# Where the mixer steps stand beside the expert pairs: a hybrid mLSTM, attention and PEER layer on one core

## The chip, the core and the metric

The kernel runs on one core of one Trainium2 chip. The metric is device time in microseconds. The kernel before took 3650.06 us (median of 3 runs, 3642.83 to 3653.0). All data is float32.

## The reference

One layer is computed for 128 context tokens and 1024 latent tokens (model width 1024), which are nine tiles of 128 tokens. For each token x:

```
h  = modulate(rmsnorm(x), c)
x1 = x + gate1 * [ mLSTM(h) | attention(h) ] @ w_out      # mLSTM: 4 heads of 128, both directions; attention: 8 heads of 64
h2 = modulate(rmsnorm(x1), c)
q  = h2 @ w_q                                             # 1024 x 2048: 8 heads, two halves of 128
sa, sb = q[:, half 0] @ sub_a.T, q[:, half 1] @ sub_b.T   # 128 scores each
(va, ia), (vb, ib) = top_k(sa, 16), top_k(sb, 16)
top, pos = top_k(va + vb over all 256 sums, 16)           # 16 experts a head, 128 a token
e  = ia[..] * 128 + ib[..];  gates = softmax(top)
y  = x1 + gate2 * sum over the 128 experts of  gates * gelu(h2 . u[e]) * v[e]
```

The attention of a latent token goes to its neighbours within 128 tokens and to 128 cached context keys. The mLSTM runs over the latent tiles forwards and backwards, with a state that is carried from tile to tile. u and v are tables of 16384 rows of 1024; 147,456 rows of each are gathered, 1208 MB in all, and this is most of the memory traffic.

## The kernel before, in words

There are three programs one after the other. `conditioning` and `project_in` make the modulation and h @ w_in for all tiles, and put q, k, v and the heads into DRAM scratch. `mix_and_experts` (from line 658) does the rest. It is the only one that the change touches, apart from four semaphores that it takes over from `conditioning`.

`mix_and_experts` has one program for each engine. Every program is written by the same generator `drive` out of five kinds of pieces, so that the order of the pieces is the same on all engines, and each engine works in its own order:

- `mlstm()`: 18 units (two directions, nine tiles), each in three steps, and a last round of three: 57 cell steps. A unit loads q and k turned, k, v and the sums of the gates (`load_cell`). The sums are broadcast to all partitions and land in the same buffer `ew` in which ACT then makes their exponentials.
- `mixer(t)`: 15 steps (`SUBS`) for a tile. In steps 0 to 8 even steps write the scores of two heads and weigh the values of two (PE), and odd steps take the minimum (DVE), the exponential (ACT) and the turn (PE) of two heads. Step 4 adds the mLSTM outputs of both directions and squares them (POOL), steps 5 to 8 norm them. Step 9 turns the mix, steps 10 to 13 multiply by w_out, and steps 12 and 14 add to x and give x1. Step 14 stores x1.
- `route(t)`: 51 steps for a tile: the norm of x1, sixteen query products with chunks of w_q in two halves, the scores of the sub-keys, and then on DVE the top 16 of 16 lists of 128 and of 8 lists of 256, and the expert numbers and gates. `choose` does this in two parts of 4 heads; after each part the semaphore `s_route` rises and POOL may fetch the experts of these heads.
- `pair(t, r)`: 64 pairs for a tile. A pair is two gathers by POOL (a row of u and v for every token), two dot products with h2 on DVE, gelu and weights on ACT, and the weighted sum of the v rows on PE. The ring holds 8 gathers, so POOL issues the gathers of pair n+4 when PE has done pair n.
- `begin()`: waits until all mLSTM units are stored, then issues the first gathers.

In the lead-in `drive` issues 6 cell steps, the 15 steps of the context mixer with 7 cell steps, and 34 routing steps of tile 0 with 44 cell steps (`PART`, `cells_beside`). After `begin`, after each `pair(t, r)` it issues `pace(t, r)` routing steps and a mixer step if `due(t, r)` says so. Before, the mixers of tiles 1 to 8 (120 steps) take 49 steps in expert tile 0, 41 in tile 1 (17 of them beside its pairs 0 to 27) and 30 in tile 2, never more than one a pair. Expert tile 0 has 51 routing steps.

w_q comes in chunks of 512 KB. For the first three tiles (`STREAMED`) every tile's queries read 16 chunks that SP loads anew: into four buffers in the first half of tile 0, into two after that. At pair 30 of tile 2 (`WQ_AT`), when all mixers are done, w_q is loaded whole (8.39 MB) into the space that the mixers leave, and all later queries read it there.

## Time and profile before

| | |
|---|---|
| median of 3 runs | 3650.06 us |
| the profiled execution: time, span | 3663.39 us, 3661.7 us |
| first gather issued | 630.4 us |
| first expert pair of tiles 0, 1, 2, 3, 4 on DVE | 639.3, 1007.1, 1377.3, 1727.6, 2048.4 us |
| PE, DVE, ACT, POOL busy | 72%, 67%, 27%, 40% of the span |
| gathers: 1208.03 MB | 79.0% of the time of 16 DMA engines |
| all DMA | 1368.53 MB, mean 374 GB/s |

Matmuls and the other instructions are named by engine, line and tiles (`fx_acc<-fx_ring`, the expert matmul, reads the gathered rows); a buffer's number is left out. A float32 matmul of 512 columns shows as two records. Busy time is that of an engine's instructions, the DMA share is the mean over 16 DMA engines, and the clock is that which TensorE was granted, as a share of the full 2.4 GHz. Stages are cut at the first dot product that ends a tile's pair; pairs 28 of tiles 1 and 2 are at 1161.3 and 1530.8 us.

### The profile page before, as it was taken

To read this page: it belongs to the slowest core of one execution; us is meant where nothing else is said; L and a number is where in the kernel's file an instruction comes from. 1 tells how busy PE (TensorE), PEld (TensorE's weight loads), DVE (VectorE), ACT (ScalarE), POOL (GpSimd) and SP (SyncE) were. 2 spreads that over 40 slices of the span, in tenths; PEclk is the share of its full clock that TensorE was granted. 3 is DMA by queue.
4 is the path that set the end of the run, shared out by engine and by line. 5 is a ranking of instruction groups with operands and counts; after the bars stand their busy time and mean duration, and the time that the engine had idled before them with its cause. 6 is when DMAs were issued, how large, how long until landed. Compare 5 with 4: busy or idle time off the path is not lost.

```text
span 3661.7 us, 30563 instructions
## 1 busy us (share of the span) xinstructions
PE 2650.2 (72%) x9522; PEld 1018.7 (28%) x9522; DVE 2444.6 (67%) x5512; ACT 984.9 (27%) x2685; POOL 1462.5 (40%) x1298
## 2 busy tenths in 40 slices
PE   7999786888868888766576667557656755675555
PEld 3455455333323333322122112112211211221111
DVE  3665446857685768648867667686766768676655
ACT  1223233443433244412122122112212211221111
POOL 0110023443553444534444444444444444444443
PEclk9999888899888989988788779778977977987777
DMA  7222467999999999999999999999999999999998
GB/s 300 94 99 95 164 201 229 403 416 425 394 427 402 409 391 416 416 424 413 427 427 423 427 423 427 420 421 427 417 427 417 427 419 424 426 418 426 417 427 366
DMA packets 233359, 1368.53 MB, mean 374 GB/s; under 512 B 25422, under 2 KB 45530, under 8 KB 84714
## 3 DMA queue, kind: packets, MB, share of 16 engines
q0 software_dynamic: 165888, 1208.03, 79.0%
q1 hardware_dynamic: 60104, 138.71, 10.5%
q10 hardware_dynamic: 7204, 19.84, 1.4%
q8 instruction: 75, 1.23, 0.1%
q14 instruction: 88, 0.72, 0.0%
HBM read 1337.99 MB, written 28.50 MB: 373 GB/s over the span
## 4 chain that ended last, share of the span: by engine, by line
DMA 40%; PE 21%; DVE 15%; POOL 4%; issue 4%; ACT 3%; SPq 1%; ACTq 0%; POOLq 0%; DVEq 0%
DMA fx_ring<-arg_uv,fx_eidx 36%; PE fx_acc L1456 12%; DVE fx_ring L1941 8%; POOL fx_ring L1142 4%; PE at_sP L1299 3%; ACT fx_weighted_pick L1614 2%; DMA rt_wq<-arg_w_q 2%; PE rt_qP L1327 1%; PE at_aP L1235 1%; DMA ml_e<-gate_cum_scratch 1%; DVE rt_rest L1794 1%; DVE rt_ab L1796 1%; DVE rt_rest L1792 1%; DMA rt_w_q<-arg_w_q 1%; ACT fx_gelu L1610 1%
## 5 line engine op out<-in xcount | busy, mean ns | idle before, releaser
L1456 PE MATMUL fx_acc<-fx_ring,fx_weighted_pick 128*64 128x512 f32 x4608 | 1456.2, 765 | 886.6 <-ACT fx_weighted_pick L1614 854.8
L1142 POOL DMA_INDIRECT fx_ring<-arg_uv,fx_eidx x1152 | 1322.9, 1148 | 1647.4 <-PE fx_acc L1456 1450.1
L1941 DVE CUSTOM_DVE_ANT_0 fx_ring<-fx_ring,fx_h 128x1024 f32<-128x1024 f32 x1152 | 1405.7, 1233 | 750.3 <-DMA fx_ring<-arg_uv,fx_eidx 743.7
L1456 PEld LDWEIGHTS fx_acc<-fx_ring,fx_weighted_pick 128*64 128x64 f32 x4608 | 332.5, 161 | 1879.7 <-ACT fx_weighted_pick L1614 1310.9
L1610 ACT ACTIVATE fx_gelu<-fx_dot 128x2 f32<-128x2 f32 x576 | 117.1, 203 | 2094.7 <-DVE fx_dot L1941 2079.8
L429 PE MATMUL in_z<-w_in,in_hT 128*128 128x512 f32 (+1 forms) x864 | 352.7, 566 | 9.0 <-PEq L97 9.0
L1614 ACT ACTIVATE fx_weighted_pick<-fx_weighted_pick,fx_gelu 128x64 f32<-128x64 f32 x1152 | 338.2, 340 | 55.1 <-ACT fx_gelu L1610 2.2
L429 PEld LDWEIGHTS in_z<-w_in,in_hT 128*128 128x128 f32 x864 | 163.9, 193 | 179.1 <-issue 173.8
L1327 PE MATMUL rt_qP<-rt_w_q,rt_h2T 128*128 128x512 f32 x384 | 198.5, 642 | 10.0 <-DMA rt_w_q<-arg_w_q 10.0
L389 POOL COPY in_turned<-in_heads 128x320 f32<-128x320 f32 x9 | 9.1, 1009 | 320.9 <-DVE in_heads L584 320.9
L1299 PE MATMUL at_sP<-at_w_out,at_mixT 128*128 128x512 f32 x288 | 135.7, 615 | 0.9 <-DVE at_mixT L1687 0.9
L1327 PEld LDWEIGHTS rt_qP<-rt_w_q,rt_h2T 128*128 128x128 f32 x384 | 69.1, 200 | 145.7 <-issue 134.2
L1933 DVE TENSOR_TENSOR fx_weighted_pick<-fx_pick,fx_gates 128x512 f32<-128x512 f32 x144 | 99.4, 690 | 1.8
L1632 DVE CUSTOM_DVE_ANT_0 at_s<-at_sP,at_mask,at_sink_negated 128x512 f32<-128x512 f32 x64 | 47.2, 750 | 76.0 <-PE at_sP L1219 65.0
L1941 DVE DVE_READ_ACCUMULATOR2_ANT fx_dot<- 128x1 f32 x1152 | 94.8, 82 | 0.0
L1610 ACT ACT_TABLE_LOAD x64 | 82.1, 1283 | 1.1
L1327 PE MATMUL rt_qP<-rt_wq,rt_h2T 128*128 128x512 f32 x128 | 68.5, 661 | 16.9 <-DMA rt_wq<-arg_w_q 16.9
L1299 PEld LDWEIGHTS at_sP<-at_w_out,at_mixT 128*128 128x128 f32 x288 | 54.1, 197 | 80.7 <-issue 80.7
L636 DVE SCALAR_TENSOR_TENSOR in_ada_acc<-in_ada_w,silu,in_ada_acc 128x1024 f32<-128x1024 f32 x56 | 70.1, 1293 | 0.3
L1175 POOL TENSOR_TENSOR ml_k<-ml_k,ml_cols 128x512 f32<-128x512 f32 x18 | 18.7, 1039 | 114.6 <-ACT ml_cols L1580 62.5
L1219 PE MATMUL at_sP<-att_kT,at_qT 64*128 64x384 f32 x128 | 59.8, 551 | 0.0
L1235 PE MATMUL at_aP<-att_v,at_pT 128*128 128x64 f32 x384 | 57.5, 289 | 0.0
(324 smaller groups left out, 2375.6 us busy)
## 6 DMA issues: line engine op xcount, KB each, us to landing
rt_wq<-arg_w_q SPq DMA_DIRECT2D x44, 512.0 KB, 8.0
fx_ring<-arg_uv,fx_eidx POOLq DMA_INDIRECT x1152
in_ada_w<-arg_w_ada SPq DMA_DIRECT2D x32, 512.0 KB, 4.2
ml_qkT<-qkT_scratch SPq DMA_DIRECT2D x18, 512.0 KB, 4.3
ada_w<-arg_w_ada SPq DMA_DIRECT2D x8, 1024.0 KB, 13.4
w_in<-arg_w_in SPq DMA_DIRECT2D x16, 512.0 KB, 16.9
rt_w_q<-arg_w_q SPq DMA_DIRECT2D x16, 512.0 KB, 38.4
kv_scratch<-in_kv ACTq DMA_DIRECT2D x9, 768.0 KB, 3.3
```

The costliest lines, as they stand in the source:

```text
L429: mm = pe.matmul(zp[b % 3][:, 0:n], hT[par][:, k, :], g.w_in[:, k, c0:c0 + n], start=(k == 0), stop=(k == KD - 1))
L636: dve.scalar_tensor_tensor(ada_acc[cnd][:], ada_w[m % AW][:], g.silu[:, k, cnd:cnd + 1], ada_b[:] if k == 0 else ada_acc[cnd][:], ALU.mult ...
L1142: pool.indirect_dma_start(out=ring[j][:], out_offset=None, in_=io.uv, in_offset=bass.IndirectOffsetOnAxis(ap=eidx[t % 2][:, i:i + 1], axis=0),
L1219: pe.matmul(ST[h % 2][:, P:4 * P], lhs, g.akT[half, t * P:t * P + 3 * P], start=True, stop=True).then_inc(s_sc, 1)
L1235: mm = pe.matmul(aP[:, h * ADH:(h + 1) * ADH], pT[h % 2][:, j * P:(j + 1) * P], rhs, start=(j == 0), stop=(j == 3))
L1299: mm = pe.matmul(ST[half][:], mixT[:, j, :], w_out[:, j, half * 512:(half + 1) * 512], start=(j == 0), stop=(j == KD - 1))
L1327: mm = pe.matmul(banks[half][b][:], hq2T[:, k, :], w[:, b * 512:(b + 1) * 512], start=(k == 0), stop=(k == KD - 1))
L1456: mm = pe.matmul(acc[b][cg * TOKS:(cg + 1) * TOKS, :], wsel[:, i % (2 * FILL), :], ring[i % GROUP][:, D + b * 512:D + (b + 1) * 512], star ...
L1610: act.activation(gelu[:, sl], dot[:, sl], ACT.Gelu_apprx_tanh).then_inc(s_gelu, 1)
L1614: last = act.activation(wsel[:, i, :], wsel[:, i, :], ACT.Copy, scale=gelu[:, i:i + 1])
L1933: dve.tensor_tensor(wsel[:, lo:lo + FILL, :], pick[:].unsqueeze(1).to_broadcast([P, FILL, TOKS]), gates[t % 2][:, r * NC:r * NC + FILL].un ...
L1941: dve.tensor_tensor_reduce(out=ring[j][:, 0:D], in0=ring[j][:, 0:D], in1=h2r[t % 2][cg][:], scale=1.0, scalar=0.0, op0=ALU.mult, op1=ALU.a ...
```

## The change

The gate sums get buffers of their own (`eb`), and are loaded by `load_sums` ahead of the rest of a unit (unit 3 excepted). w_out and the first gate1 are issued by SP in the second mLSTM unit instead of before the first. The lead-in has 30 routing steps instead of 34, with the same 44 cell steps beside them. Tile 0 is routed in three parts of 2, 2 and 4 heads and has 60 routing steps. The second half of its queries has four w_q buffers, two of them the mix and its turned copy, which the mixers don't need between tiles 0 and 1. Expert tile 0 gets a mixer step after every pair (64) and 64 routing steps, tile 1 gets two mixer steps after each of pairs 0 to 27 (56), and from then on there are none. Only the queries of tiles 0 and 1 stream w_q; it is loaded whole at pair 28 of tile 1. The diff, cut to its core:

```diff
@@ -670,11 +671,11 @@
     TURN = 6
     ROWS = TURN + 11
     PART = TURN + 28
-    FOLD = PH // 2 * TOPK
+    LEAD_STEPS = TURN + 24
     HQ = NSIDE // 2
-    WQ_AT = 30
+    WQ_AT = 28
     WQ = 2
-    STREAMED = 3
+    STREAMED = 2
     HALF = NSIDE // 2 * P
     FILL = 8
...
     def second(t):
-        return TURN + 14 if t else PART - 11
-
-    def picks(t, hh):
-        return max(PART, second(t) + 11) if hh else TURN + 11
+        return TURN + 14 if t else LEAD_STEPS - 11
+
+    def parts(t):
+        return ((0, 2), (2, 2), (4, 4)) if t == 0 else ((0, 4), (4, 4))
+
+    def routed(t, i):
+        return i + 1 + (t * 2 + 1 if t else 0)
+
+    def pieces(heads):
+        return 9 + 2 * heads
+
+    def picks(t, i):
+        if i == 0:
+            return TURN + 11
+        after = picks(t, i - 1) + pieces(parts(t)[i - 1][1])
+        return max(after, second(t) + 11) if parts(t)[i][0] == PH // 2 else after
+
+    def steps_ahead(t):
+        return PART if t else LEAD_STEPS
 
     def steps_of(t):
-        return picks(t, 1) + PART - TURN - 11
+        return picks(t, len(parts(t)) - 1) + pieces(PH // 2)
...
     def due(t, r):
-        if t == STREAMED - 1:
-            return r < WQ_AT
-        return t == 0 and r < SUBS or 17 <= r < 23 or r >= 51 or r % 2
+        return (1, 2 * int(r < WQ_AT))[t] if t < STREAMED else 0
 
     def pace(t, r):
         if t == STREAMED - 1:
             return int(r < 17 or r >= WQ_AT - 1) + int(r >= 48 and r % 2)
-        return 1
-
-    def ahead(m):
-        return 2 * WQ if m < HQ else WQ
+        return 1 + int(t == 0 and r % 8 == 2)
+
+    def buffer_of(m):
+        if m < HQ:
+            return m % 4
+        if m < NSIDE:
+            return (0, 1, 4, 5)[m % 4]
+        return m % WQ
+
+    def before(m):
+        return max((i for i in range(m) if buffer_of(i) == buffer_of(m)), default=None)
+
+    def loads(m):
+        return sum(buffer_of(i) == buffer_of(m) for i in range(m + 1))
 
     def cells_beside(k):
-        return 2 if TURN + 11 <= k < TURN + 21 else 1
+        return 2 if TURN + 4 <= k < TURN + 18 else 1
...
-        for k in range(PART):
+        for k in range(LEAD_STEPS):
             for _ in range(cells_beside(k)):
                 next(cells, None)
             next(steps)
...
         for t in range(TILES):
-            left = steps_of(t) if t + 1 < TILES else steps_of(t) - PART
+            left = steps_of(t) - steps_ahead(t) + (PART if t + 1 < TILES else 0)
             for r in range(PAIRS):
                 pair(t, r)
                 for _ in range(min(pace(t, r), left)):
                     next(steps)
                     left -= 1
-                if due(t, r):
+                for _ in range(due(t, r)):
                     next(subs, None)
...
+        wq += [mix[:], mixT[:].rearrange("p k n -> p (k n)")]
...
@@ -960,6 +988,8 @@
                     if t == 1:
                         for d in range(2):
                             sp.wait_ge(s_hst[d], 16 * (TILES - 1))
+                    if t == 1:
+                        sp.wait_ge(s_qd, NSIDE)
                     if t:
...
                             sp.wait_ge(s_x1, t * 2 + 2)
                             sp.dma_start(g.x1_dram[t], x1[:]).then_inc(s_x1o, 16)
                             if t == 0:
+                                chunk(HQ + 2)
+                                chunk(HQ + 3)
                                 sp.dma_start(gate1[:], g.gate_dram[1:1 + 1, :].to_broadcast([P, D])).then_inc(s_g1, 16)
...
                 def chunk(m):
                     if m < NSIDE * STREAMED:
-                        if m >= ahead(m):
-                            sp.wait_ge(s_qd, m - (2 * WQ if m < HQ + WQ else WQ) + 1)
+                        if before(m) is not None:
+                            sp.wait_ge(s_qd, before(m) + 1)
                         k, half = m % KD, m // KD % 2
-                        i = m % ahead(m)
-                        sp.dma_start(wq[i][:], io.w_q[k * P:(k + 1) * P, half * HALF:(half + 1) * HALF]
+                        i = buffer_of(m)
+                        sp.dma_start(wq[i], io.w_q[k * P:(k + 1) * P, half * HALF:(half + 1) * HALF]
                                      ).then_inc(s_wq[i], 16)
...
-                            if m < HQ - WQ:
-                                chunk(m + 2 * WQ)
-                            elif m >= HQ:
-                                chunk(m + WQ)
+                            for later in range(m + 1, m + 7):
+                                if before(later) == m:
+                                    chunk(later)
...
                 def load_cell(u):
                     t, d = divmod(u, 2)
                     ti = tiles(t)[d]
+                    if u != 3:
+                        load_sums(u)
                     if t:
                         sp.wait_ge(s_o, u * 2 - 2)
                         sp.wait_ge(s_cd, u * 2 - 2)
...
                                  ).then_inc(s_ld[d], 16)
+                    if u == 3:
+                        load_sums(u)
+
+                def load_sums(u):
+                    t, d = divmod(u, 2)
+                    ti = tiles(t)[d]
...
-                    sp.dma_start(ew[d][:], g.cum_dram[d:d + 1, :, ti * P:(ti + 1) * P].to_broadcast([P, MH, P])
-                                 ).then_inc(s_ld[d], 16)
+                    if t:
+                        sp.wait_ge(s_e, u - 1)
+                    sp.dma_start(eb[d][:], g.cum_dram[d:d + 1, :, ti * P:(ti + 1) * P].to_broadcast([P, MH, P])
+                                 ).then_inc(s_eb[d], 16)
 
                 def mlstm():
                     for u in range(UNITS + 1):
                         if 0 < u < UNITS - 1:
                             load_cell(u + 1)
+                        if u == 1:
+                            sp.dma_start(gate1[:], g.gate_dram[0:0 + 1, :].to_broadcast([P, D])).then_inc(s_g1, 16)
+                            for k in range(KD):
+                                sp.dma_start(w_out[:, k, :], io.w_out[k * P:(k + 1) * P, :]).then_inc(s_wo, 16)
...
                              allow_slow_non_contiguous=True).then_inc(s_small, 16)
                 load_h(0)
                 sp.dma_start(x1[:], io.x[0]).then_inc(s_x, 16)
-                sp.dma_start(gate1[:], g.gate_dram[0:0 + 1, :].to_broadcast([P, D])).then_inc(s_g1, 16)
-                for k in range(KD):
-                    sp.dma_start(w_out[:, k, :], io.w_out[k * P:(k + 1) * P, :]).then_inc(s_wo, 16)
                 drive(begin, pair, mixer, route, mlstm)
...
                 def fetch(n):
                     t, r = divmod(n, PAIRS)
-                    if r % (PAIRS // 2) == 0:
-                        pool.wait_ge(s_route, t * 2 + 1 + r // (PAIRS // 2))
+                    for i, (first, heads) in enumerate(parts(t)):
+                        if r == first * TOPK // NC:
+                            pool.wait_ge(s_route, routed(t, i))
...
+                            i = buffer_of(m)
+                            pe.wait_ge(s_wq[i], wq_base[i] + 16 * loads(m))
+                            w = wq[i]
...
-                        act.wait_ge(s_ld[d], u // 2 * 64 + 64)
+                        act.wait_ge(s_eb[d], ADA_LOADS + u // 2 * 16 + 16)
+                        if u >= 2:
+                            act.wait_ge(s_o, u * 2 - 2)
                         for h in range(MH):
-                            last = act.activation(ew[d][:, h, :], ew[d][:, h, :], ACT.Exp, bias=cols[d][:, 0, h:h + 1])
+                            last = act.activation(ew[d][:, h, :], eb[d][:, h, :], ACT.Exp, bias=cols[d][:, 0, h:h + 1])
...
                 def choose(t):
                     c = cr
                     at = 0
-                    for hh in range(2):
-                        while at < picks(t, hh):
+                    for i, (first, heads) in enumerate(parts(t)):
+                        while at < picks(t, i):
                             at += 1
                             yield
-                        for _ in half_chosen(c, t, hh):
+                        for _ in chosen(c, t, i, first, heads):
                             at += 1
                             yield
...
-                def half_chosen(c, t, hh):
-
-                    HH = PH // 2
-                    hs4 = slice(HH * hh, HH * hh + HH)
-                    lists = slice(2 * HH * hh, 2 * HH * (hh + 1))
-                    part = slice(hh * FOLD, (hh + 1) * FOLD)
-                    for b in (2 * hh, 2 * hh + 1):
+                def chosen(c, t, i, first, heads):
+
+                    hs4 = slice(first, first + heads)
+                    lists = slice(2 * first, 2 * (first + heads))
+                    part = slice(first * TOPK, (first + heads) * TOPK)
+                    for b in range(first // 2, (first + heads) // 2):
                         dve.wait_ge(s_cs, t * NG + (b + 1))
                         yield from top16(c, range(4 * b, 4 * b + 4), sc, srest, val, idx)
...
-                    h3 = flat.rearrange("p (q b) -> p q b", b=TOPK)
-                    h4 = flat.rearrange("p (h a b) -> p h a b", h=HH, b=TOPK)
+                    used = flat[:, 0:heads * TOPK * TOPK]
...
-                            ins = dve.scalar_tensor_tensor(to[:, hh * KS:(hh + 1) * KS, cg], of[:, 0, :, half], float(P),
+                            ins = dve.scalar_tensor_tensor(to[:, pairs, cg], of[:, 0, :, half], float(P),
                                                            of[:, 1, :, half], ALU.mult, ALU.add)
```

## Rows read from the trace of the kernel before

**Rows 1.** The page: chain that ended last, by line; costliest groups, gather issues
```profile
DMA fx_ring<-arg_uv,fx_eidx 36%; PE fx_acc L1456 12%; DVE fx_ring L1941 8%; POOL fx_ring L1142 4%; PE at_sP L1299 3%; ACT fx_weighted_pick L1614 2%; DMA rt_wq<-arg_w_q 2%; PE rt_qP L1327 1%; PE at_aP L1235 1%; DMA ml_e<-gate_cum_scratch 1%; DVE rt_rest L1794 1%; DVE rt_ab L1796 1%; DVE rt_rest L1792 1%; DMA rt_w_q<-arg_w_q 1%; ACT fx_gelu L1610 1%
...
L1142 POOL DMA_INDIRECT fx_ring<-arg_uv,fx_eidx x1152 | 1322.9, 1148 | 1647.4 <-PE fx_acc L1456 1450.1
```

**Rows 2.** Stages: us, busy us per engine (count), PE clock, DMA share, GB/s
```profile
639.30:1007.10 367.80, 308.33 (x1246) 134.42 (x1247) 262.59 (x609) 148.73 (x347) 169.25 (x141) 0.90 1.00 410
1007.10:1161.30 154.20, 118.99 (x432) 48.42 (x430) 117.61 (x281) 59.55 (x142) 72.28 (x60) 0.84 1.01 424
1161.30:1377.30 216.00, 184.66 (x726) 78.81 (x724) 139.52 (x318) 71.85 (x177) 93.20 (x81) 0.88 0.97 395
1377.30:1727.60 350.30, 261.38 (x1032) 103.13 (x1032) 248.79 (x577) 117.45 (x296) 163.83 (x137) 0.88 1.01 417
1530.80:1727.60 196.80, 132.06 (x486) 44.29 (x484) 124.75 (x283) 44.60 (x135) 82.91 (x73) 0.86 1.00 415
1727.60:2048.40 320.80, 211.61 (x696) 59.81 (x696) 227.91 (x520) 69.39 (x222) 144.01 (x129) 0.81 1.01 426
500.00:620.00 120.00, 97.27 (x603) 75.93 (x601) 67.33 (x251) 44.92 (x149) 38.32 (x52) 0.91 0.70 227
```

**Rows 3.** Chain of waits before the first gather: start us, us, what
```profile
442.06 13.54 DMA ml_e<-gate_cum_scratch
...
456.96 1.39 ACT at_s L1477 x8
...
487.50 6.87 PE at_sP L1299 x16
...
503.43 6.17 DMA ml_e<-gate_cum_scratch
...
577.65 4.96 DMA ml_e<-gate_cum_scratch
...
599.93 8.12 DMA rt_wq<-arg_w_q
...
619.23 1.12 DVE rt_rest L1792
...
626.13 1.23 DVE rt_ab L1796
```

**Rows 4.** Timeline of DVE: the row maximum of the context mixer
```profile
454.67 0.17 DVE L1645 TENSOR_TENSOR at_negmax<-at_max,at_sink_negated 128x8 f32<-128x8 f32 x1
```

**Rows 5.** DMA issues from 420 to 640 us: last column, median us to landing
```profile
ml_v<-kv_scratch SPq DMA_DIRECT2D x18, 256.0 KB, 5.2
ml_e<-gate_cum_scratch SPq DMA_DIRECT2D x18, 256.0 KB, 6.2
```

**Rows 6.** Timeline of expert pairs beside attention: start us, us, engine, line, tiles
```profile
1379.76 3.68 PE L1456 MATMUL fx_acc<-fx_ring,fx_weighted_pick 128*64 128x512 f32 x8 [3.73 <-DVE fx_h L1915]
...
1389.01 1.22 DVE L1941 CUSTOM_DVE_ANT_0 fx_ring<-fx_ring,fx_h 128x1024 f32<-128x1024 f32 x1
...
1390.57 0.59 ACT L1614 ACTIVATE fx_weighted_pick<-fx_weighted_pick,fx_gelu 128x64 f32<-128x64 f32 x2
...
1390.69 1.62 PE L1225 MATMUL at_sP<-ident,at_s 128*128 128x128 f32 x8
...
1392.24 1.94 PE L1456 MATMUL fx_acc<-fx_ring,fx_weighted_pick 128*64 128x512 f32 x8
...
1394.11 0.43 PE L1235 MATMUL at_aP<-at_cache_v,at_pT 128*128 128x64 f32 x2
...
1396.03 0.48 PE L1218 MATMUL at_sP<-at_cache_kT,at_qT 64*128 64x128 f32 x2
...
1397.23 0.81 PE L1219 MATMUL at_sP<-att_kT,at_qT 64*128 64x384 f32 x2
...
1398.07 0.75 DVE L1632 CUSTOM_DVE_ANT_0 at_s<-at_sP,at_mask,at_sink_negated 128x512 f32<-128x512 f32 x1
```

**Rows 7.** Groups by line, 639.3 to 1551 us: POOL squares the mLSTM output
```profile
L1122 POOL TENSOR_TENSOR at_h_square<-at_mix 128x512 f32<-128x512 f32 x8 | 10.1, 1258 | 0.6
```

57 lines of the change are left out of this document (30 added, 27 removed).

## The prediction

> **What bounds the kernel now.** The chain that ended last comes first: it puts 36% of the span on the gathers of expert rows and 12% on the expert matmuls [rows 1]. Where that holds is read next, from the busy time cut at the first expert pair of each tile [rows 2]. From 639.3 us on, the DMA engines are busy for 0.97 to 1.01 of every stage. Expert tile 3, which has no mixer beside it, takes 320.8 us at 426 GB/s, 5.01 us a pair. Tiles 0, 1 and 2 carry mixers and streamed w_q, and they take 367.8, 370.2 (154.2 + 216.0) and 350.3 us. PE is busy for 308 of the 367.8 us of tile 0, so it is the next engine in line. Before 639.3 us there are no gathers, and all that is ahead of them is paid in full: I read the chain from 440 to 634 us [rows 3]. It walks through PE, ACT and DVE and stops at loads of the gate sums (13.54 us once, then four waits from 6.17 to 4.96 us, 25.5 us in all) and once at a w_q chunk (8.12 us). PE is busy for 97 of the 120 us from 500 to 620 [rows 2].
>
> **The change, part by part.** The sum is made against this execution, span 3661.7 us and time 3663.4.
>
> *Lead-in.* (a) The gate sums get a buffer of their own and are asked for ahead of q, k and v. The wait of 13.54 us ends at 455.6; with it gone the exponentials of the context mixer (456.96) still need the row maximum, which DVE has at 454.84 [rows 3, 4]. That is late next: 2 us saved, not 13. w_out is issued some 4 us later, behind unit 2's loads (439 instead of 435). It is 4.2 MB, 10 us at the 410 GB/s of tile 0 [rows 2], and its first use comes after those exponentials, so I cost it nothing; without that cover it would cost the 4 us. (b) Of the four later waits, v becomes the last to land: its median is 5.2 us against 6.2 for the sums [rows 5], and one issue less goes ahead of it, about 0.5 us; with the shorter queue I take 2 us for each of three. At the first of them (503 us) two w_q chunks (1 MB, 2.5 us at 410 GB/s) are now queued ahead on SP, which takes it back. 6 us. (c) The second half of w_q has four buffers instead of two, which hides most of the 8.12 us: 6. (d) The first part picks for 2 heads, not 4. Its last six operations run from 619.23 to 627.36 [rows 3]; half of that is 4 us. Smaller top-16 work earlier on DVE: 3 us. The mLSTM units are neither fewer nor cheaper (44 cell steps lie beside 30 steps instead of beside 34). Sum: 21 us. Bounds: 54 if all five sum waits, the w_q wait, (d) and the 3 us go whole; nothing, if later w_out and earlier chunks give back what is won.
>
> *Expert tile 0.* It gets 64 mixer steps instead of 49, and 64 routing steps beside them, 13 more than 51. Fifteen mixer steps are one mixer, which loads and stores 2.05 MB: 5.0 us at the stage's 410 GB/s. DVE has the 2-head part and its shorter pieces more. Gathers of pairs 16 on wait for the second part (done in pair 10, needed in pair 12), and those of pair 32 on for the third (done in pair 26, needed in pair 28), so POOL doesn't stop. Lower bound +5. Upper bound: PE 308 + 38 for the mixer = 346 us, at 0.9 of the time 385, which is +17. I take +9.
>
> *Expert tile 1, pairs 0 to 27*, 154.2 us now, with 17 mixer steps. This stage gets 56, two after every pair. That is where the change is decided, for DVE, ACT and PE each work in program order and the expert pair is put between the mixer steps. Where an even and an odd attention step share a pair, the cycle is closed: PE writes the scores of two heads, DVE must take the minimum of the second (0.75 us and the read) before it may do the next pair's two dot products (1.22 us each), ACT then does gelu and weights (0.9 us to 1391.16), PE the pair (1.94 us), the values of two heads (1394.11 to 1396.03) and the next scores (to 1398.04) [rows 6]. 0.8 + 2.4 + 0.9 + 1.9 + 1.9 + 2.0 = 10.0 us, against 5.0 for the gathers of a pair. With one step a pair, as now, the dot products of the next pair run during the scores, and the DMA hides all of it. Where the steps fall odd then even, the turn and the values lie on one pair: scores, 0.8, exponential 1.0, turn of the second head 0.5, copy 0.6, its values 1.0, scores 2.0, with the pair in between: 6.5. A w_out double step is 16 matmul records of 0.43 us (16 in 6.87 us [rows 3]) and the pair, 8.8. Steps 13 and 14 in one pair put the x1 addition ahead of the dot products: 10.3. Steps 8, 9 with POOL's two passes and the turn of the mix: 7. With 6 for steps 14 and 0, the rest of tile 5's mixer is 20 + 7.5 + 17.6 + 6 = 51, tile 7's 8 + 30 + 7.5 + 17.6 + 6 = 69, those of tiles 6 and 8 each 19.5 + 6 + 7 + 8.8 + 10.3 = 52. That is 223 us for the 28 pairs at the higher PE clock. PE's part of it runs at a granted clock of 0.84 to 0.91 in these stages [rows 2]: 12 us more. 235 us, +81. Lower bound: nothing in the chain but PE's own work (187, in the rivals), +33. Upper: every pair a closed cycle of 10 us, 280, +126.
>
> *Tile 1, pairs 28 to 63.* No mixers, no streamed chunks; w_q's 8.39 MB load here. Its likeness is tile 2 from pair 28 on, with the same load from pair 30: 196.8 us, against 216.0 [rows 2]: -19. The wait of the first resident query is in that row.
>
> The load is 8.39 MB and the 16 chunks that go are as much; at the 426 GB/s of tile 3 [rows 2] that is 19.7 us. The Trainium skill ("DMA: Bandwidth & Descriptors", "Where 436 GB/s comes from") takes about 358 GB/s for a core's reads of HBM, which would make it 23.4 us; the row is above that limit, so the measurement decides, and the sum uses neither.
>
> *Tile 2.* Loses its mixers, chunks and w_q load and becomes tile 3: 350.3 to 320.8, -29.5. From tile 3 on nothing changes.
>
> Sum: -21 + 9 + 81 - 19 - 29.5 = +20.5 us. The median shown is 3650.06, 13.3 below the profiled execution; the difference is laid on the median: 3670.
>
> **Rivals.**
> A. *PE packs the doubled steps*, and the stage costs PE's work alone. 28 pairs at 1.94 are 54 us. A mixer at the higher clock is w_out 32 x 0.43 = 13.7, scores 4 x 2.0 = 8.0, values 4 x 1.9 = 7.7, turns 4 x 1.1 (1.62 at a mixed clock [rows 6]) and the mix 1.1: 35; 3.73 mixers are 131 us. 54 + 131 = 185 and some 2 for gaps: 187, +33. Total -21 + 9 + 33 - 48.5 = -27.5: 3622. For it: PE was busy 0.84 of tile 0, and a pair's eight matmul records take 1.94 us at the clock's level of 2.4 GHz against 3.68 at 1.2 [rows 6], so that more of the higher level would pay. Against it: the closed cycle above, in which PE waits for DVE. The Trainium skill ("TensorE: Matmul & The Clock Gate", "HAM oscillation") has it that idle gaps bring the clock down and steady work keeps it up; by that rule doubled steps would pay back part of their price. The trace agrees in direction: the granted clock is 0.91 from 500 to 620 us, where PE is busy 97 of 120 us, and 0.81 in tile 3, where it is busy 212 of 321 [rows 2].
> B. *Every pair of the stage is a closed cycle*, not only those that hold an even and an odd step. POOL issues two gathers of 1.15 us [rows 1] after each pair and ahead of its mixer passes of 1.26 us [rows 7], and DVE waits for POOL's square before its next dot products; in pairs 0 to 16 a routing piece lies on DVE ahead of the minimum too. At 9.9 us a pair the stage is 277 us, +123: 3650 - 21 + 9 + 123 - 48.5 = 3712. It decides where POOL's result is later than DVE's minimum. Against it: POOL's part touches steps 4, 5, 8 and 9 of fifteen, and the routing piece is short enough to lie under PE's pair in most.
> C. *The lead-in gains nothing*: the waits for sums turn into waits for q, k and v, which can't be asked for before the unit before last is done, and the tail is all that goes, 4 us. 3650 + 20.5 + 17 = 3687. For it: PE is already busy 97 of 120 us.
> D. *The lead-in gains double* (42 us, PE clock up, DVE out of the way): 3650 - 0.5 = about 3650. For it: the five sum waits and the w_q wait are 47 us together.
>
> **How the numbers follow.** Forecast 0.45, A 0.20, B 0.12, C 0.13, D 0.10. About 0.3% (11 us) is what a measurement of this kernel can tell from no change. A is faster; D is the same, and the forecast's lower side, with 7.5 a pair and D's half, shares its place: 0.18 in all for no change. Faster 0.22 with a little of D mixed with A. Slower 0.60. The likeliest case alone spans 3648 to 3695. The range holds A's end and most of B: 3616 to 3706.
>
> **What would show it.** First gather at about 609 us instead of 630.4; no wait for gate sums on the chain but one, and v's load in their place. Tile 0 at 373 to 385 us with the DMA at 1.0. In pairs 0 to 27 of tile 1 the DMA busy share falls to about 0.7 and the chain goes through scores, DVE's minimum, dot products and PE instead of through gathers; about 8.4 us a pair. Pairs 28 to 63 near 197 and tile 2 near 321 us. The prediction is wrong if that stage stays below 200 us, or if the lead-in gains over 35.

## The result: 2.5% slower, and where the time went

The changed kernel takes 3736.06 us (median of 4 runs, 3732.76 to 3755.33) against 3646.93 (4 runs on the same chip, 3642.83 to 3653.0): ratio 1.0247, 95% interval 1.0222 to 1.0271. The forecast was 3670 us with a range of 3616 to 3706. Its sign was right and its size was not: the loss is 89 us, where 20 were forecast.

The page of the changed kernel, the chain that ended last by line (the chain is followed back from the last instruction; the shares are of the whole span), and the group of the gathers:

```profile
DMA fx_ring<-arg_uv,fx_eidx 40%; PE fx_acc L1496 10%; DVE fx_ring L1984 6%; POOL fx_ring L1185 4%; ACT fx_weighted_pick L1657 2%; PE at_sP L1342 1%; DVE rt_rest L1837 1%; DVE rt_ab L1839 1%; DVE rt_rest L1835 1%; ACT fx_gelu L1653 1%; PE at_aP L1278 0%; PE at_sP L1262 0%; PE at_sP L1261 0%; DVE at_xn L1738 0%; DVE fx_dot L1984 0%
...
L1185 POOL DMA_INDIRECT fx_ring<-arg_uv,fx_eidx x1152 | 1299.0, 1128 | 1756.3 <-PE fx_acc L1496 1563.7
```

The two rows answer to [rows 1]. POOL's idle time ahead of a gather went from 1647 to 1756 us, all of the growth put down to the expert matmul: gathers are issued later because PE is late with the pair that frees the ring. The gathers' share of the chain rose from 36 to 40%, but that is not to be read as "more DMA bound", and it says nothing about the stage that grew. The chain of the changed kernel, followed back from its end, stops at 1026 us, and in pairs 0 to 27 of tile 1 it does not pass through a gather at all. The chain of that stage alone (1013 to 1278 us):

```profile
by line: PE fx_acc L1496 19.7%; PE at_sP L1342 19.1%; DVE fx_ring L1984 11.0%; issue 11.0%; PE at_aP L1278 6.7%; PE at_sP L1262 3.7%; ACT fx_weighted_pick L1657 2.8%; POOL fx_ring L1185 2.5%; PE at_sP L1261 1.7%; DVE at_xn L1738 1.6%; DVE a
```

It goes through the expert matmul, the w_out product (`at_sP L1342`), DVE's dot products and the attention matmuls. In the kernel before, the gathers are the largest item of the chain in the same pairs, 40 of 154 us. The rise of the total comes from the later stages, where the chain now passes through gathers more often: from pair 28 of tile 1 to the end of tile 2 they are 300 us of it, where they were 90.

The stages of the changed kernel: stretch, us, busy us of PE, PE's weight load, DVE, ACT and POOL (count), granted PE clock, DMA share, GB/s.

```profile
629.30:1013.30 384.00, 324.37 (x1414) 151.28 (x1415) 285.11 (x707) 177.54 (x388) 167.91 (x144) 0.95 0.98 394
1013.30:1278.40 265.10, 219.25 (x852) 107.45 (x850) 144.73 (x347) 104.72 (x216) 79.97 (x74) 0.85 0.73 274
1278.40:1472.50 194.10, 130.63 (x470) 44.09 (x472) 123.59 (x281) 44.72 (x135) 79.13 (x70) 0.83 0.99 407
1472.50:1793.80 321.30, 205.77 (x700) 58.47 (x696) 227.65 (x519) 69.30 (x222) 143.44 (x128) 0.83 1.01 427
500.00:620.00 120.00, 94.65 (x625) 73.64 (x624) 64.10 (x217) 48.75 (x155) 39.59 (x53) 0.97 0.71 235
805.40:861.50 56.10, 49.92 (x230) 25.86 (x229) 27.75 (x58) 30.75 (x65) 25.23 (x21) 0.97 0.97 395
1077.10:1107.20 30.10, 27.32 (x153) 16.42 (x153) 25.89 (x67) 25.41 (x47) 12.65 (x11) 0.94 0.92 348
1147.50:1184.40 36.90, 26.70 (x122) 14.27 (x122) 21.38 (x47) 19.68 (x38) 7.99 (x8) 0.78 0.49 182
```

Against [rows 2]: in the second row, pairs 0 to 27 of tile 1, the DMA share is 0.73 where it was 1.01, and the stage takes 265.1 us where it took 154.2. Nothing else in the table comes near that. PE is busy for 219 of the 265 us and DVE for 145, so neither is full: something goes round in a circle. In this text a circle, or closed cycle, is a chain of operations on several engines whose end is what its beginning waits for. The third and fourth rows are back on the DMA engines (0.99 and 1.01). The sixth row is pairs 32 to 39 of tile 0, 7.0 us a pair, where PE is busy for 49.9 of 56.1 us (0.89) and the DMA share is 0.97: both are near full. The last two are an odd-then-even stretch and an even-then-odd stretch of tile 1, with a DMA share of 0.92 and 0.49.

| step | forecast | measured in the two profiled executions |
|---|---|---|
| lead-in, to the first pair | -21 | 639.3 to 629.3: -10.0 |
| tile 0 | +9 | 367.8 to 384.0: +16.2 |
| tile 1, pairs 0 to 27 | +81 | 154.2 to 265.1: +110.9 |
| tile 1, pairs 28 to 63 | -19 | 216.0 to 194.2: -21.8 |
| tile 2 | -29.5 | 350.3 to 321.3: -29.0 |
| tile 3 to the end | 0 | 1934.0 to 1937.1: +3.1 |
| sum | +20.5 | +69.3 |

The rest of the 89 us lies in which executions were profiled. The execution profiled before lies 16 us above its median, that of the changed kernel (3732.76) 3 us below.

Who waits for whom in pairs 0 to 27 of tile 1 (us in total, times, longest), the kernel before and then the changed one:

```profile
ACT fx_gelu L1610 <- DVE fx_dot L1941: 85.8, 27, 7.2
POOL fx_ring L1142 <- PE fx_acc L1456: 67.3, 25, 5.3
...
DVE fx_ring L1941 <- DMA fx_ring<-arg_uv,fx_eidx: 20.2, 15, 2.5
```

```profile
POOL fx_ring L1185 <- PE fx_acc L1496: 173.8, 29, 9.9
ACT fx_gelu L1653 <- DVE fx_dot L1984: 102.6, 20, 12.5
...
PEld fx_acc L1496 <- ACT fx_weighted_pick L1657: 34.7, 17, 5.6
```

ACT's and POOL's waits are there in both. What tells them apart is the last row of the first fence, DVE waiting for gathered rows, which is the sign of a bound by DMA: in this stage of the changed kernel there is no such wait, not one. The other is POOL's wait for PE: 29 times up to 9.9 us, instead of 25 times up to 5.3.

One turn of the circle, from the timeline of the changed kernel (start us, us, engine, line, operation; in brackets the idle time and what ended it):

```profile
1159.63 3.32 PE L1496 MATMUL fx_acc<-fx_ring,fx_weighted_pick 128*64 128x512 f32 x8 [1.70 <-ACT fx_weighted_pick L1657]
...
1162.87 0.43 PE L1278 MATMUL at_aP<-at_cache_v,at_pT 128*128 128x64 f32 x2
...
1164.80 0.49 PE L1261 MATMUL at_sP<-at_cache_kT,at_qT 64*128 64x128 f32 x2
...
1166.00 0.81 PE L1262 MATMUL at_sP<-att_kT,at_qT 64*128 64x384 f32 x2
...
1166.84 0.75 DVE L1675 CUSTOM_DVE_ANT_0 at_s<-at_sP,at_mask,at_sink_negated 128x512 f32<-128x512 f32 x1
...
1167.85 0.69 DVE L1706 TENSOR_REDUCE at_hrms<-at_h_square 128x4 f32<-128x512 f32 x1 [0.26 <-POOL at_h_square L1164]
...
1168.65 0.68 DVE L1976 TENSOR_TENSOR fx_weighted_pick<-fx_pick,fx_gates 128x512 f32<-128x512 f32 x1
1169.26 1.22 DVE L1984 CUSTOM_DVE_ANT_0 fx_ring<-fx_ring,fx_h 128x1024 f32<-128x1024 f32 x1
...
1170.40 1.22 DVE L1984 CUSTOM_DVE_ANT_0 fx_ring<-fx_ring,fx_h 128x1024 f32<-128x1024 f32 x1
...
1171.95 0.59 ACT L1657 ACTIVATE fx_weighted_pick<-fx_weighted_pick,fx_gelu 128x64 f32<-128x64 f32 x2
...
1172.59 1.97 PE L1496 MATMUL fx_acc<-fx_ring,fx_weighted_pick 128*64 128x512 f32 x4 [3.43 <-ACT fx_weighted_pick L1657]
```

Read from top to bottom: the pair on PE, the values of two heads, the next scores, DVE's minimum (which stands in the program ahead of the next dots), DVE's norm of the mLSTM output (which waits 0.26 us for POOL's square), the filling of the weights, the two dot products, the weights on ACT, and only now the next pair: 12.96 us for a pair that costs the DMA engines 5. The turn goes over PE, DVE and ACT, with POOL at its side, and no step of it waits for a gather.

### The profile page after: what moved, and what is told of

It is laid out like the page before. It is cut to its first block, busy times and chain, and to the rows that moved or that the text cites. A ratio compares the mean times of both kernels' runs of the same rounds, so it can differ in the third digit from the quotient of the medians.

```text
span 3731.0 us, 30573 instructions
## 1 busy us (share of the span) xinstructions
PE 2643.4 (71%) x9522; PEld 1008.5 (27%) x9522; DVE 2445.9 (66%) x5534; ACT 983.0 (26%) x2684; POOL 1432.1 (38%) x1298
## 4 chain that ended last, share of the span: by engine, by line
DMA 40%; PE 13%; DVE 9%; POOL 4%; issue 4%; ACT 3%; ACTq 0%; POOLq 0%; DVEq 0%
DMA fx_ring<-arg_uv,fx_eidx 40%; PE fx_acc L1496 10%; DVE fx_ring L1984 6%; POOL fx_ring L1185 4%; ACT fx_weighted_pick L1657 2%; PE at_sP L1342 1%; DVE rt_rest L1837 1%; DVE rt_ab L1839 1%; DVE rt_rest L1835 1%; ACT fx_gelu L1653 1%; PE at_aP L1278 0%; PE at_sP L1262 0%; PE at_sP L1261 0%; DVE at_xn L1738 0%; DVE fx_dot L1984 0%
## 5 line engine op out<-in xcount | busy, mean ns | idle before, releaser
L1185 POOL DMA_INDIRECT fx_ring<-arg_uv,fx_eidx x1152 | 1299.0, 1128 | 1756.3 <-PE fx_acc L1496 1563.7
L1367 PE MATMUL rt_qP<-rt_w_q,rt_h2T 128*128 128x512 f32 x448 | 225.6, 627 | 0.0
L430 PEld LDWEIGHTS in_z<-w_in,in_hT 128*128 128x128 f32 x864 | 163.6, 192 | 176.2 <-issue 170.8
L1342 PE MATMUL at_sP<-at_w_out,at_mixT 128*128 128x512 f32 x288 | 134.7, 616 | 4.9 <-DVE at_mixT L1730 4.9
L1367 PEld LDWEIGHTS rt_qP<-rt_w_q,rt_h2T 128*128 128x128 f32 x448 | 78.0, 194 | 152.2 <-issue 152.2
L1653 ACT ACT_TABLE_LOAD x62 | 79.5, 1283 | 1.1
L1342 PEld LDWEIGHTS at_sP<-at_w_out,at_mixT 128*128 128x128 f32 x288 | 54.0, 196 | 83.3 <-issue 83.3
L1738 DVE TENSOR_TENSOR at_xn<-at_sP,at_gate 128x512 f32<-128x512 f32 x18 | 12.5, 692 | 80.7 <-PE at_sP L1342 80.5
L1527 ACT ACTIVATE at_s<-at_s,at_negmax 128x512 f32<-128x512 f32 x64 | 46.0, 719 | 69.6 <-DVE at_negmax L1675 69.1
```

The lines of the kernel that those rows point to most:

```text
L430: mm = pe.matmul(zp[b % 3][:, 0:n], hT[par][:, k, :], g.w_in[:, k, c0:c0 + n], start=(k == 0), stop=(k == KD - 1))
L1185: pool.indirect_dma_start(out=ring[j][:], out_offset=None, in_=io.uv, in_offset=bass.IndirectOffsetOnAxis(ap=eidx[t % 2][:, i:i + 1], axis=0),
L1342: mm = pe.matmul(ST[half][:], mixT[:, j, :], w_out[:, j, half * 512:(half + 1) * 512], start=(j == 0), stop=(j == KD - 1))
L1367: mm = pe.matmul(banks[half][b][:], hq2T[:, k, :], w[:, b * 512:(b + 1) * 512], start=(k == 0), stop=(k == KD - 1))
L1653: act.activation(gelu[:, sl], dot[:, sl], ACT.Gelu_apprx_tanh).then_inc(s_gelu, 1)
```

## Experiments

Ratios are to the kernel before on the same chip, with 95% intervals. Stage lengths are those of one profiled execution each.

| kernel | ratio | tile 0 | tile 1, pairs 0 to 27 | tile 1 | tile 2 |
|---|---|---|---|---|---|
| before | 1 | 367.8 | 154.2 | 370.2 | 350.3 |
| changed | 1.0247 | 384.0 | 265.1 | 459.3 | 321.3 |
| lead_only | 0.9999 (0.9987 to 1.001) | 366.6 | 150.8 | 357.6 | 350.8 |
| stage_only | 1.0212 (1.0188 to 1.0235) | 370.8 | 262.0 | 456.4 | 321.2 |
| odd_first | 1.0182 (1.0156 to 1.0207) | 384.0 | 228.4 | 434.0 | 321.1 |
| even_first | 1.0381 (1.035 to 1.0411) | 390.0 | 296.3 | 501.8 | 321.1 |
| dots_ahead | 1.0227 (1.021 to 1.0244) | 390.7 | 230.6 | 432.9 | 320.8 |
| dots_ahead_one_table | 1.0155 (1.0133 to 1.0176) | 394.2 | 220.7 | 421.3 | 321.2 |
| pe_kept_busy | 1.0267 (1.0237 to 1.0297) | 387.5 | 272.3 | 468.1 | 319.6 |
| ends40 | 1.0203 (1.0184 to 1.0222) | 387.8 | 200.5 | 431.1 | 321.6 |
| ends40_dots_ahead | 1.0159 (1.014 to 1.0178) | 387.8 | 188.5 | 424.3 | 321.0 |
| one_a_pair | 1.0126 (1.0094 to 1.0158) | 393.3 | 170.5 | 392.5 | 341.8 |
| one_a_pair_late | 1.0088 (1.0066 to 1.0111) | 369.8 | 163.6 | 399.9 | 341.4 |

**lead_only and stage_only: the change cut in two.** The first is the changed kernel with the mixer schedule of before; the second is the kernel before with the new schedule alone.

```diff
 lead_only: changed kernel
-    WQ_AT = 28
-    STREAMED = 2
+    WQ_AT = 30
+    STREAMED = 3
     def due(t, r):
-        return (1, 2 * int(r < WQ_AT))[t] if t < STREAMED else 0
+        if t == STREAMED - 1:
+            return int(r < WQ_AT)
+        return int(t == 0 and r < SUBS or 17 <= r < 23 or r >= 51 or r % 2 == 1)
```

> The changed kernel with the mixer schedule and the w_q streaming of before (three streamed tiles, w_q whole at pair 30 of tile 2); what stays is the new lead-in and the three parts of tile 0. Theory (the loss is all in pairs 0 to 27 of tile 1): first gather at about 619 us as in the changed kernel, tile 0 within 5 us of 368, all later stages as before; about 10 us under the kernel before, ratio 0.997. Rival (the new lead-in or the three parts cost something in tile 0): ratio 1.00 or above, tile 0 over 378 us.

> The kernel before with only the mixer schedule changed: two streamed tiles, w_q whole at pair 28 of tile 1, two mixer steps after each of pairs 0 to 27, one a pair in tile 0. Theory: this alone is the loss. First gather at 630, pairs 0 to 27 of tile 1 about 265 us, tile 0 some 10 us longer than 368; ratio 1.025 to 1.030. Rival (part of the loss comes from the lead-in's part of the change): ratio under 1.02.

The schedule alone costs 74 us (1.0212, between the theory's 1.025 and the rival's bound of 1.02); its interval just overlaps that of the whole change (1.0247). What is left of the 89 us, if anything is, belongs to neither half alone: tile 0 takes 384.0 us with both halves and 366.6 and 370.8 with one. The new lead-in with the three-part routing is worth nothing that can be measured in time: 3649.79 us (10 runs) against 3651.59 (13), where 10 us were expected. The profiles do show something. In the eleven kernels with the new lead-in the first pair comes at 628.5 to 635.5 us, 631.5 on average; in the two with the old one at 639.3 (before) and 635.8 (stage_only). So it comes some 6 us earlier, and one profile of each kernel is not enough to say more.

**odd_first and even_first: the same 56 steps, the other way round.** Both spread them over 30 pairs; the one puts the odd step of attention first in a pair, (1,2), (3,4), ..., the other the even one, (0,1), (2,3), ...

```diff
 both: changed kernel, WQ_AT = 30
-        return (1, 2 * int(r < WQ_AT))[t] if t < STREAMED else 0
+        if t == 0:
+            return 1
 odd_first:
+        return (1 if r % 8 == 6 or r == 0 else 2) if t == 1 and r < WQ_AT else 0
 even_first:
+        return (1 if r % 8 == 5 else 2) if t == 1 and r < WQ_AT else 0
```

> The changed kernel with the 56 mixer steps of tile 1 over 30 pairs, step 0 of a mixer alone and then 1 and 2, 3 and 4, up to 13 and 14; w_q whole at pair 30. Theory (a pair that holds an even step and then an odd one makes a closed cycle through PE's scores, DVE's minimum and DVE's dot products): about 8 us a pair, 30 pairs in 235 to 245 us. Rival (PE's own work, the same in both orders, sets the stage): equal to its counterpart with even steps first.

> The same with steps 0 and 1, 2 and 3, up to 12 and 13 together and step 14 alone; as many pairs (30) and the same 56 steps. Theory: about 10.8 us a pair, 30 pairs in 315 to 330 us, 70 to 90 us above its counterpart with odd steps first. Rival: equal to it.

```profile
1013.40:1262.50 249.10, 210.49 (x869) 104.32 (x867) 147.37 (x353) 110.00 (x224) 85.85 (x78) 0.91 0.82 305
```

```profile
1022.70:1339.90 317.20, 255.03 (x868) 125.30 (x866) 148.95 (x353) 105.57 (x222) 81.35 (x77) 0.74 0.62 231
```

These are pairs 0 to 29 of tile 1 in odd_first, then in even_first: 249.1 and 317.2 us for the same instructions in another order, the DMA share 0.82 and 0.62. 68 us of span, and 71 us between the medians, lie between two kernels that do the same work, so the cost is neither PE's nor DVE's amount of work. The theory had 235 to 245 and 315 to 330 us; the rival, equal times, is out. The clock takes part in the difference: for the same matmuls PE is busy for 210.5 us at a granted clock of 0.91, and for 255.0 us at 0.74. How much of the 68 us would be left at an equal clock was not measured. Half of the changed kernel's mixers go one way and half the other, and its 269.7 us for these pairs lie between the two.

**dots_ahead: DVE's dots ahead of the mixer's minimum.** In tile 1 DVE does the dot products of the next pair before the mixer steps. Only DVE's program is written with `early=True`; PE, ACT and POOL keep their order.

```diff
             for r in range(PAIRS):
-                pair(t, r)
+                if not (early and t == 1 and 0 < r <= WQ_AT):
+                    pair(t, r)
                 for _ in range(min(pace(t, r), left)):
                     next(steps)
                     left -= 1
+                if early and t == 1 and r < WQ_AT:
+                    pair(t, r + 1)
                 for _ in range(due(t, r)):
                     next(subs, None)
...
-                drive(begin, pair, mixer, route, mlstm)
+                drive(begin, pair, mixer, route, mlstm, early=True)
```

> The changed kernel with one thing moved on DVE alone: beside pairs 0 to 27 of tile 1, DVE does the two dot products of pair r+1 ahead of its parts of the mixer steps that follow pair r. The work and all other engines' orders stay. Theory (the closed cycle runs through DVE's minimum ahead of the next dot products): pairs with an even and an odd step fall from about 12 to 8 us, pairs 0 to 27 from 265 to about 210 us, ratio to the kernel before 1.008 to 1.013. Rival (PE's work, or POOL's, bounds the stage): 255 us or more, ratio 1.02 or above.

From PE's start of pair 0 to that of pair 27 it took 228.2 us, where the changed kernel took 253.9: a gain in this stage, and far less than the expected one (about 210 for a stage of 265). In time it is not clear of noise: 1.0227 against 1.0247, with intervals that overlap. In the profiled execution tile 0, whose code is the same, took 6.7 us more and gave back part of the gain. The timeline shows a second circle under the first:

```profile
1160.44 0.81 PE L1265 MATMUL at_sP<-att_kT,at_qT 64*128 64x384 f32 x2
...
1161.28 0.75 DVE L1678 CUSTOM_DVE_ANT_0 at_s<-at_sP,at_mask,at_sink_negated 128x512 f32<-128x512 f32 x1
...
1162.08 0.72 ACT L1530 ACTIVATE at_s<-at_s,at_negmax 128x512 f32<-128x512 f32 x1
...
1162.91 1.28 ACT L1656 ACT_TABLE_LOAD   x1
...
1164.21 0.20 ACT L1656 ACTIVATE fx_gelu<-fx_dot 128x2 f32<-128x2 f32 x1
...
1164.50 0.59 ACT L1660 ACTIVATE fx_weighted_pick<-fx_weighted_pick,fx_gelu 128x64 f32<-128x64 f32 x2
...
1165.14 1.94 PE L1499 MATMUL fx_acc<-fx_ring,fx_weighted_pick 128*64 128x512 f32 x8 [1.54 <-ACT fx_weighted_pick L1660]
```

The minimum no longer stands ahead of the dots, but the exponential of the mixer stands on ACT ahead of the gelu: scores, minimum, exponentials, a table load of 1.28 us, gelu, weights, pair, values, scores. A pair with an even and then an odd attention step takes 9.4 to 11.7 us, where it took 11.4 to 13.0. This second circle is there because ACT kept its old order; what is left when gelu and weights also go ahead of the exponential on ACT was not tried.

**dots_ahead_one_table: is the table load a link?** ACT copies the dots in pairs 0 to 27 of tile 1 instead of taking their gelu, so this kernel leaves out a part of the function; of the 32 table loads in this stage 9 are left.

```diff
-                    act.activation(gelu[:, sl], dot[:, sl], ACT.Gelu_apprx_tanh).then_inc(s_gelu, 1)
+                    f = ACT.Copy if t == 1 and r < WQ_AT else ACT.Gelu_apprx_tanh
+                    act.activation(gelu[:, sl], dot[:, sl], f).then_inc(s_gelu, 1)
```

> The kernel with VectorE's dot products moved ahead of the mixer steps in the second expert tile, and in the same 28 pairs ScalarE copies the dots where it computed their gelu (28 of the 576 pairs lack the function). In that stretch the exponential and the gelu no longer take turns, so the 1.28 us table load that stands between the exponential and the gelu goes. Theory: with the dots ahead, the even-then-odd stretch is held by a second closed cycle, scores -> minimum -> exponential -> table load -> gelu -> weights -> TensorE's pair -> values -> scores, and the load is a link of it. Then each of some 14 such pairs is 1.3 us shorter (9.4 to 11.7 us become 8 to 10.4), the first PE start to the 28th comes down from 228 us to 205 to 213, tile 1 from 433 to 410 to 418, and the ratio from 1.023 to 1.017 to 1.019. Rival: another link (POOL's square of the queries, the gather) holds these pairs, and the load has slack: tile 1 430 to 436, ratio 1.021 to 1.024.

```profile
1153.99 0.81 PE L1265 MATMUL at_sP<-att_kT,at_qT 64*128 64x384 f32 x2
...
1155.63 0.72 ACT L1530 ACTIVATE at_s<-at_s,at_negmax 128x512 f32<-128x512 f32 x1
...
1156.35 0.19 ACT L1657 ACTIVATE fx_gelu<-fx_dot 128x2 f32<-128x2 f32 x1
...
1156.63 0.59 ACT L1661 ACTIVATE fx_weighted_pick<-fx_weighted_pick,fx_gelu 128x64 f32<-128x64 f32 x2
...
1157.27 1.94 PE L1499 MATMUL fx_acc<-fx_ring,fx_weighted_pick 128*64 128x512 f32 x8
```

From the last scores' matmul to the next pair it is now 3.3 us (1153.99 to 1157.27) where it was 4.7 (1160.44 to 1165.14). The six pairs 13 to 18 took 62.4 us with the load and 53.9 without, 1.4 us less a pair, and the four at the stage's start 41.5 and 38.3, 0.8 less a pair. Of the 8.5 us in the six pairs, 3.5 lie in the expert matmuls themselves, fewer of which ran at the lower clock. Tile 1 fell by 11.6 us against 15 to 23 expected; the ratio fell more than expected, from 1.0227 to 1.0155. So the load is a link of the second circle; I had counted on more of the 28 pairs. The Trainium skill ("ScalarE: Activation LUTs", "What ACT_TABLE_LOAD costs") gives 1283 ns for the load and about 2.7 us for a switch of tables, drain included. The trace agrees on the load (1.28 us) and not on the drain: in the rows of dots_ahead above the load starts at 1162.91 and the gelu behind it at 1164.21, so the whole switch takes 1.3 us here, and the measurement decides.

**pe_kept_busy: the clock.** In the changed kernel PE's eight records of a pair span the lower level of the clock (1.2 GHz, 3.3 to 3.7 us instead of 1.94) in 12 of these 28 pairs; in odd_first it is 7, in even_first 20, and in the kernel before 8, where the DMA hides them. The experiment puts four matmuls of 512 columns, whose result nobody reads, into an idle PSUM bank at the head of eight of the waiting pairs. Three waits stand ahead of the first of them, so that the bank has been read; PE did not stand idle at them.

```diff
+                    if t == 1 and r == 1:
+                        pe.wait_ge(s_qT, 2 * NG)
+                        pe.wait_ge(s_h2a, 2 * NC)
+                        pe.wait_ge(s_h2d, 2 * NC)
+                    if t == 1 and r in (1, 2, 3, 14, 15, 16, 17, 18):
+                        for _ in range(4):
+                            pe.matmul(qP[0][:], g.ident[:], g.akT[:, 0:512], start=True, stop=True)
                     if t and r == 0:
                         pe.wait_ge(s_gated, t * 2)
```

> The changed kernel with four more matmuls of 512 columns, whose result nobody reads, ahead of the wait for the weights of pairs 1 to 3 and 14 to 18 of tile 1, where PE stands idle after steps of the even-then-odd kind. Theory (PE's idle time takes the granted clock to 1.2 GHz and the pair's eight records to 3.7 us; this is the term that my forecast left out): these pairs' records fall to about 1.9 us, and the stage gets 8 to 14 us shorter though PE does more. Rival (the clock is not set by PE's idle time here, or PE is not on the cycle): records stay at 3.3 us and more, and the stage is the same or longer.

```profile
1020.00:1292.30 272.30, 237.30 (x912) 118.35 (x912) 146.66 (x345) 104.51 (x215) 83.49 (x73) 0.90 0.70 265
```

The granted clock of pairs 0 to 27 rose from 0.85 to 0.90, and only 2 pairs were left at the lower level. The stage had been expected to get 8 to 14 us shorter and did not (272.3 us against 265.1, one profile each; the ratios' intervals overlap). The added work stands in the circle itself: ahead of pair 1 the extra matmuls run from 1036.05 to 1040.90 us and the pair starts at 1040.83. The Trainium skill ("TensorE: Matmul & The Clock Gate", "HAM oscillation") says that waits bring the clock down and that busy time holds it up. The granted clock agrees in direction. Single waits do not settle it: after 1.70 us of waiting a pair took 3.32 us in the changed kernel, after 1.54 us another took the full-speed 1.94 in dots_ahead. This filler could not buy the clock's cost back.

**ends40 and ends40_dots_ahead: the 56 steps over 40 pairs**, w_q whole at pair 40.

```diff
-    WQ_AT = 28
+    WQ_AT = 40
-        return (1, 2 * int(r < WQ_AT))[t] if t < STREAMED else 0
+        if t == 0:
+            return 1
+        return 1 + int(r % 5 in (1, 3)) if t == 1 and r < WQ_AT else 0
-            return int(r < 17 or r >= WQ_AT - 1) + int(r >= 48 and r % 2)
+            return int(r < 17 or r >= WQ_AT - 1) + int(WQ_AT + 5 <= r < WQ_AT + 19)
```

> The changed kernel with the 56 mixer steps of tile 1 spread over pairs 0 to 39 (one a pair, two in 16 of them), w_q whole at pair 40, and two routing steps of tile 2 a pair from pair 45 to 58. Theory: the pairs with one step stay with the DMA (5.8 us), the sixteen double ones cost 7 to 11 us, so the 40 pairs take 270 to 290 us and tile 1 about 405 to 425 us against 370 of before; tile 2 at 321; ratio 1.000 to 1.008. Rival (doubling is cheap if it is sparse): tile 1 under 395, ratio under 0.998.

> Both: the mixer steps over 40 pairs and DVE's dot products of the next pair ahead of the mixer parts. Theory: what the doubled pairs cost goes mostly; the 40 pairs take 235 to 255 us, tile 1 370 to 390, ratio 0.992 to 0.998, which would be the first version under the kernel before. Rival: no better than the spread alone.

The 40 pairs themselves took 287.1 us, within the 270 to 290 expected. Pairs 0 to 27 fall to 200.5 us, but 28 to 63 rise from 194.2 to 230.6, since the mixers and the next tile's routing now lie there: tile 1, 431.1 us, misses the expected 405 to 425 and gains 28 us of the 89 that it lost. With the dots ahead the 40 pairs took 272.2 us (235 to 255 expected) and tile 1 gains 7 more, to 424.3, where I had expected 370 to 390 and a kernel faster than before. Fewer double pairs are cheaper, but no spacing that was tried gets the 56 steps into tile 1 for the 29 us that tile 2 gives back.

**one_a_pair and one_a_pair_late: never two steps in a pair.** w_q is loaded in tile 2 as before.

```diff
 both: changed kernel, WQ_AT = 30, STREAMED = 3
 one_a_pair:
+        return int(t == 0 or t == 1 and r < PAIRS - 8)
 one_a_pair_late:
+        if t == 2:
+            return int(r < WQ_AT)
+        return int(t == 1 or r < SUBS or 17 <= r < 23 or r >= 51 or r % 2 == 1)
```

> The new lead-in with one mixer step in each pair of the first expert tile (64) and in each of the first 56 pairs of the second; none in the third, where w_q is loaded at pair 30 as before. Theory: what costs is a second step that stands between TensorE's pair and the next dots; with one step a pair every minimum finds a pair of dots between it and the last one, so nothing closes: tile 1 350 to 370 us (357.6 with 41 steps), tile 0 384 as in the changed kernel, tile 2 343 to 351; ratio 0.999 to 1.007. Rival: the cost goes by the number of steps in the tile, whatever their spacing (the changed kernel pays (459.3 - 357.6) / 15 more steps = 6.8 us a step): tile 1 450 and ratio 1.02 or over.

> The new lead-in, the first expert tile with its 49 mixer steps of before, the second with one step in each of its 64 pairs, the third with the 7 that are left. Theory: tile 0 366 to 371 us, where fewer pairs meet both a step and routing than in the changed kernel (384); tile 1 353 to 373; tile 2 343 to 351; ratio 0.996 to 1.003, so about as the kernel before. If tile 0's 384 us come from the number of steps in it and tile 1 can take 64 at the same price, tile 1 grows by 17 us over 357.6 instead, to 375, and the ratio is 1.001 to 1.005.

Neither theory of tile 1 held. It took 392.5 and 399.9 us: 15 more steps than in lead_only cost 34.9 us, 23 more cost 42.3, so 1.8 to 2.3 us a step, where doubled steps cost (459.3 - 357.6) / 15 = 6.8 and I had written nearly nothing. Tile 0 of one_a_pair_late, with 49 steps, took 369.8 us, as expected. The waits of one_a_pair in pairs 16 to 31, and the timeline of one of them:

```profile
POOL fx_ring L1185 <- PE fx_acc L1496: 62.1, 16, 9.7
DVE at_s L1675 <- PE at_sP L1262: 34.2, 5, 11.4
```

```profile
1197.54 1.28 ACT L1527 ACT_TABLE_LOAD   x1
...
1200.03 3.68 PE L1367 MATMUL rt_qP<-rt_wq,rt_h2T 128*128 128x512 f32 x4 [2.69 <-DMA rt_wq<-arg_w_q]
...
1205.37 0.49 PE L1261 MATMUL at_sP<-at_cache_kT,at_qT 64*128 64x128 f32 x2
...
1206.55 0.75 DVE L1675 CUSTOM_DVE_ANT_0 at_s<-at_sP,at_mask,at_sink_negated 128x512 f32<-128x512 f32 x1 [9.94 <-PE at_sP L1262]
...
1207.31 1.94 PE L1496 MATMUL fx_acc<-fx_ring,fx_weighted_pick 128*64 128x512 f32 x8
```

DVE waits five times, up to 11.4 us, for scores. On PE a query product stands ahead of those scores: PE waits 2.69 us for a streamed chunk of w_q, and the product runs at the lower clock (3.68 us). With a step in every pair each minimum waits for scores that stand behind a query product. On odd pairs alone, as before, every other pair is free to catch up. The circle is closed here through w_q's DMA, over two pairs instead of one. That the chunk is the decisive link in all of them was read from the trace, not tried by itself.

No kernel that was run is faster than the one before; lead_only equals it.

## Why the forecast had the sign and not the size

**Lead-in, -21: measured -10.0 in the profile and nothing in the timed runs. This term failed too.** By the last mLSTM unit's product 7.6 us had been won, where (a), (b), (c) and the 3 us of (d) had promised 17; the step that failed is above all (b), the waits for the sums. The rows show what took their place. They are the waits for DMA in the changed kernel from 440 to 629 us, and then its issues (KB each, median us to landing):

```profile
POOL ml_k L1218 <- DMA ml_v<-kv_scratch: 29.4, 5, 7.6
...
PEld fx_acc L1458 <- DMA ml_v<-kv_scratch: 8.1, 4, 3.4
```

```profile
ml_gate_sums<-gate_cum_scratch SPq DMA_DIRECT2D x18, 256.0 KB, 6.0
...
ml_v<-kv_scratch SPq DMA_DIRECT2D x18, 256.0 KB, 6.7
```

(a) The wait of 13.5 us went, and x1 of the context came 0.7 us earlier, not 2. (b) The sums no longer land last; v does, at 6.7 us where it took 5.2 [rows 5]. POOL waits 29.4 us for it in five waits; for the sums it had waited 41.8 us in seven, 12.5 of them in the wait of (a), so 29.3 in the rest: nothing saved there. This is rival C's mechanism. ACT's seven waits for the sums (11.5 us) did go. (c) PE's waits for chunks of w_q (5.1 us at its weight load) are gone; the last mLSTM unit's product is ready at 607.0 us instead of 614.6. (d) The tail to the first gather shrank from 15.8 to 12.4 us, 3.4 of the 4 forecast. The first gather came 11.0 us earlier in this profile, at 619.4, the first pair 10.0 (6 on average over all profiles), and lead_only against before showed no difference in time. That lies between the forecast and rival C, which left 4 us. Rival C had 0.13 and should have had more, by its own argument that k, q and v can't be asked for sooner.

**Tile 0, +9: measured +16.2**, and 384 to 394 us over the nine kernels that have the changed one's steps in this tile (lead_only, one_a_pair_late and stage_only do not). stage_only, with as many mixer steps but the 51 routing steps of before, took 370.8; lead_only, with the new routing and 49 mixer steps, 366.6. So it takes both. The growth is in pairs 32 to 39 and 48 to 55, 7.0 and 8.0 us a pair, where query products, routing and mixer steps meet. In the first of the two PE is busy for 0.89 of the time (the row at 805.40), and a mean over the stage hid that. In the second it is busy for 52 of 64 us (0.81) and DVE for 46, so PE is not full there, and what holds these pairs was not found. That my upper bound, which went by PE (+17), came out is therefore in part luck.

**Tile 1, pairs 0 to 27, +81: measured +110.9. This is the largest term that failed, in size.** The mechanism is the one forecast, and the two orders and the chain of the stage showed it. Cut by mixer, forecast and measured (PE start to PE start):

| mixer | pairs | forecast | measured |
|---|---|---|---|
| tile 5's rest, even then odd | 0 to 5 | 51 | 61.3 |
| tile 6, odd then even | 6 to 12 | 52 | 59.0 |
| tile 7, even then odd | 13 to 20 | 69 | 84.5 |
| tile 8, odd then even | 21 to 27 | 52 | 60.0 |

The same 28 pairs, cut by what stands in them:

| steps in a pair | pairs | forecast | measured |
|---|---|---|---|
| attention, even then odd | 6 | 58 | 73.0 |
| steps 8 and 9 | 2 | 15 | 23.5 |
| attention, odd then even | 6 | 39 | 47.8 |
| two w_out steps | 6 | 52.8 | 61.0 |
| all others | 8 | 58.6 | 59.4 |
| sum | 28 | 223.4 | 264.8 |

12 us for the clock came on top of the 223. So some 30 us are missing, and they are spread over four kinds of pairs.

*The clock was mis-sized.* I had added 12 us for it, as a mean. PE was busy for 219.3 us in this stage, and its work at the higher clock had been put at 185 (in rival A). At the granted clock of 0.85 the two agree (219.3 x 0.85 = 186), so by this estimate the clock cost PE 33 us, and in a circle that is paid in full wherever PE's work lies on it. The pairs' own records are 20 of these: 12 pairs took 3.3 to 3.7 us instead of 1.94. The chain shows one more link, in the pair that holds steps 8 and 9:

```profile
1040.52 3.68 PE fx_acc L1496 x8
1044.20 3.62 PE at_aP L1278 x16
```

The pair and its sixteen value matmuls take 7.3 us here, where the same two take 3.9 at the higher level (1.94 and 2.0). That is 3.4 of the 4.3 us by which this pair passed its forecast.

*Two sums were short.* An even-then-odd pair of attention was forecast at 10.0 us (steps 0 and 1 at 8) and took 11.4 to 13.0. In the turn shown above, of 13.0 us, 3.1 were missing from my sum: PE's pair at the lower clock (3.32 instead of 1.94, +1.4), and the 1.7 us from the minimum's end (1167.59) to the first dot (1169.26), in which DVE waits for POOL, takes the norm and fills the weights. An odd-then-even pair was forecast at 6.5 us; the terms listed for it add up to 5.9 without the expert pair and 7.8 with it, and it took 7.1 to 9.2, 8.0 on average. The second sum was the one to use.

Rival B (every pair closed, +123) was nearer in the sum and wrong in its mechanism: odd-then-even pairs stayed short, and odd_first, which has more of them, is 68 us shorter than even_first. Rival A needed the DMA or PE to be the bound of the stage, and at a DMA share of 0.73 with PE busy for 219 of 265 us neither was.

**Tile 1, pairs 28 to 63, and tile 2: -19 and -29.5, measured -21.8 and -29.0.** Taking the stage of another tile with the same load was exact to 3 us. For the first that is in part luck: its base, the 216.0 us of the execution profiled before, was long. lead_only, with the same schedule, took 206.8 us there, and against that the gain is 12.6.

**The median.** I laid the 13.3 us by which before's profiled execution lay above its median on the forecast as well. The changed kernel's lay below its own, so the timed loss came out larger than that of the spans. Against the profiled execution of lead_only, whose timed median equals before's, the changed kernel's span is 88.5 us longer, nearly the timed 89. Before's profiled span is 19.2 us longer than that of lead_only, and 12.6 of these lie in tile 1 (370.2 against 357.6).

## What to carry to other kernels

Where engines work in program order and two streams are interleaved by hand, cost a slot by the closed path through it, not by engine loads: ask of every engine what stands ahead of the instruction that the other stream waits for. Whether a pair of steps goes in as (even, odd) or (odd, even) was worth 68 us for identical work; and when one circle is opened on one engine, look for the next on the engines that kept their order (here ACT's exponential and table load) before promising its whole length. PE's lower clock is a term of such a circle and has to be costed on its links, not as a mean. And a chain followed over the whole program is to be read stage by stage: its total share can move with stages that did not matter.

## What the runs showed of the chip that was not expected

- In an even-then-odd stretch with PE busy for 26.7 of 36.9 us the mean granted clock was 0.78, and a pair's records after a wait of 1.7 us took 3.32 us, close to the 3.68 of the lower level, against 1.94. The odd-then-even stretch, with PE busy for 27.3 of 30.1 us, had 0.94.
- A switch from the exponential's table to gelu's took 1.3 us on ACT, nearly all of it the load of 1.28 us.
- The same code in tile 0 took 384.0 to 394.2 us in nine executions of kernels that differ only behind it, in which the order of its work is the same. What sets it was not found.
